# A bidirectional state-space scan rewritten: decay sums in PSUM, the output's parts accumulated in one bank by identity matmuls

## What is computed

```python
a_cs = jnp.cumsum(a, axis=2)
seg = a_cs[:, :, :, None] - a_cs[:, :, None, :]
decay = jnp.exp(jnp.where(lower, seg, -jnp.inf))
cb = jnp.einsum('bctgn,bcsgn->bctsg', cc, bc)
y_diag = jnp.einsum('bctsgh,bcsghp->bctghp', cb[..., None] * decay, xdt)
y_off = jnp.einsum('bctgn,bcghpn->bctghp', cc, h_in) * jnp.exp(a_cs)[..., None]
```

## Time and profile before

| | us |
|---|---|
| median of 3 runs | 1650.7 (1649.86 to 1651.47) |
| profiled execution | 1647.13 |
| its span, first to last instruction | 1645.4 |
| TensorE busy (matmul) | 1369.0, 83% |
| TensorE weight load busy | 1188.6, 72% |
| VectorE busy | 920.8, 56% |
| ScalarE busy | 693.6, 42% |
| GpSimd busy | 279.6, 17% |
| mean granted TensorE clock | 0.913 of 2.4 GHz |

### The profile page before, as it was taken

The page is one execution under the profiler, slowest core; times in us unless marked ns, Lnnn a source line. Parts: engine busy times, 40 slices in busy tenths (PEclk is TensorE's granted clock), DMA queues, the critical chain, the costliest instruction groups (busy, mean ns, idle before and its releaser), DMA issues. The chain is left out here.

```text
span 1645.4 us, 20520 instructions
## 1 busy us (share of the span) xinstructions
PE 1369.0 (83%) x7697; PEld 1188.6 (72%) x7697; DVE 920.8 (56%) x1201; ACT 693.6 (42%) x1186; POOL 279.6 (17%) x286
## 2 busy tenths in 40 slices
PE   3999989799998999787778734999974489999980
PEld 1799989799997889645555523998873378888860
DVE  2411532476762111288889868233346189999966
ACT  2423311244342221335557747111121177777753
POOL 0600000000000010256667741000004000000002
PEclk9999999899999999898889966999966799999995
DMA  9972211121213331511111131332435589999945
GB/s 385 406 305 77 76 53 52 59 74 57 78 52 109 118 134 72 170 52 39 39 40 40 51 140 60 115 101 92 162 153 195 201 314 408 406 412 413 413 186 204
DMA packets 55498, 267.96 MB, mean 163 GB/s; under 512 B 7467, under 2 KB 11763, under 8 KB 35062
## 3 DMA queue, kind: packets, MB, share of 16 engines
q1 hardware_dynamic: 42806, 221.21, 35.8%
q0 software_dynamic: 12608, 45.62, 7.1%
HBM read 218.54 MB, written 48.27 MB: 162 GB/s over the span
## 5 line engine op out<-in xcount | busy, mean ns | idle before, releaser
L212 PE MATMUL banks<-rounded,rounded 128*128 128x320 f32 (+1 forms) x1168 | 366.5, 314 | 20.2 <-PEq L1266 6.8
L213 PE MATMUL banks<-rounded,rounded 128*128 128x320 f32 (+1 forms) x1168 | 364.5, 312 | 0.0
L214 PE MATMUL banks<-rounded,rounded 128*128 128x320 f32 (+1 forms) x1168 | 364.4, 312 | 0.0
L191 DVE TENSOR_TENSOR rounded<-words,rounded 128x2048 fp32r<-128x2048 f32 x52 | 119.2, 2292 | 226.5 <-ACT rounded L183 224.3
L212 PEld LDWEIGHTS banks<-rounded,rounded 128*128 128x128 f32 (+1 forms) x1168 | 221.5, 190 | 21.8 <-issue 14.4
L1849 DVE TENSOR_TENSOR rounded<-words,rounded 128x2048 fp32r<-128x2048 f32 x93 | 212.9, 2290 | 34.3 <-ACT rounded L1840 33.4
L213 PEld LDWEIGHTS banks<-rounded,rounded 128*128 128x128 f32 (+1 forms) x1168 | 221.5, 190 | 0.4
L214 PEld LDWEIGHTS banks<-rounded,rounded 128*128 128x128 f32 (+1 forms) x1168 | 221.3, 189 | 0.4
L1840 ACT ACTIVATE rounded<-words 128x2048 fp32r<-128x2048 f32 x96 | 183.7, 1917 | 48.0 <-PE banks L1967 40.7
L183 ACT ACTIVATE rounded<-words 128x2048 fp32r<-128x2048 f32 x52 | 99.2, 1909 | 141.0 <-PE banks L233 62.6
L231 PE MATMUL banks<-rounded,rounded 128*128 128x512 f32 x280 | 112.1, 400 | 10.7 <-PEq L632 6.6
(11 more groups left out here) (269 smaller groups left out, 2227.7 us busy)
## 6 DMA issues: line engine op xcount, KB each, us to landing
words<-in_units SPq DMA_DIRECT2D x52, 1024.0 KB, 5.0
words<-in_wg SPq DMA_DIRECT2D x32, 1024.0 KB, 7.4
words<-in_wu SPq DMA_DIRECT2D x32, 1024.0 KB, 7.5
words<-in_wd SPq DMA_DIRECT2D x32, 1024.0 KB, 8.3
words<-in_w_mod_rest SPq DMA_DIRECT2D x32, 512.0 KB, 4.9
slot_rows<-words POOLq DMA_DIRECT2D x27, 512.0 KB, 22.9
expert_rows<-words POOLq DMA_DIRECT2D x25, 512.0 KB, 9.0
words<-in_w_mod SPq DMA_DIRECT2D x4, 2048.0 KB, 22.5
```

The source lines that it names most:

```text
L191: self.nc.vector.tensor_tensor(self.lo[:, i % 2, :], self.raw[:, i % 2, :], self.hi[:, i % 2, :].bitcast(F32), ALU.subtract).then_inc(self ...
L212: nc.tensor.matmul(out, lhs[0](k), rhs[0](k), start=(k == 0), stop=False)
L213: nc.tensor.matmul(out, lhs[0](k), rhs[1](k), start=False, stop=False)
L214: last = nc.tensor.matmul(out, lhs[1](k), rhs[0](k), start=False, stop=(k == nk - 1))
```

## The change

The scan's loop is written anew and computes the same quantities. In the diff the lines taken out of VectorE's loop, and out of ScalarE's old main loop, are left out; they stand in the listing above.

- The decays: TensorE writes into a bank for each direction first a mask of 0 and -1e30 (`shut`, through a bf16 identity), then, for each of the four heads, the running sums of `A` along the moved side: an fp32 matmul whose stationary operand is one column of `A` repeated 128 times and whose moving operand is the triangle `le` or `ge`. ScalarE takes the exponential of each head and direction, with minus the running sum (`NCS`) as its bias, into `E`. `RH`, `RL`, `AH` and the rounded triangles are gone.
- ScalarE copies the product of C and B unmasked; VectorE multiplies all eight matrices `E` of a sub-block by it in place, in one instruction. dt no longer goes into the matrix: GpSimd multiplies the rows by it, for both directions, into `XT`.
- The output of a sub-block is accumulated in one bank: the skip product through an identity matmul, eight matmuls of 64 columns (four heads, two directions), and the two scaled state terms through two identity matmuls. VectorE only scales the state terms, both in one instruction; ScalarE copies the finished bank to `X`.

```diff
-    RH, RL = kit.rnd(O_HL + 2048, 4, 512), kit.rnd(O_HL + 4096, 4, 512)
-    GX, TT = (kit.at(O_HL + 6144 + 1024 * j, 2, 512) for j in range(2))
-    M = GX
-    SO = TT
+    E = kit.at(O_HL + 2048, 6, 512)
+    XT = kit.at(O_HL + 5120, 6, 256)
+    SO = kit.at(O_HL + 6656, 2, 512)
-    gtr, ltr = kit.rnd(O_K + 1872, P), kit.rnd(O_K + 2000, P)
-    AH = kit.rnd(O_TMP + 3360, NC, 64)
+    NCS = kit.at(O_TMP + 3360, 2, NC, 32)
...
-    CB = kit.at(O_TMP + 1280, 2, 2, P)
+    CB = kit.at(O_TMP + 1280, 2, P)
+    shut = kit.at(O_TMP + 1536, P).bitcast(BF16).rearrange("p (d n) -> p d n", d=2)
+    identb = kit.at(O_TMP + 1664, P // 2).bitcast(BF16)
...
-            def decays(j):
+            def time_rows(j):
                 c, g, q = subs[j]
-                if j >= 2:
-                    pool.wait_ge(seg_done, j - 1)
-                for d, mask in ((0, le), (1, ge)):
-                    hs = heads4(g, q)
-                    av = A[:, c, 32 * d + hs.start:32 * d + hs.stop]
-                    nc.gpsimd.tensor_tensor(byhead(RL[:, 2 * d + j % 2, :], 4), av.unsqueeze(2).broadcast_to([P, 4, P]),
-                                            mask.unsqueeze(1).broadcast_to([P, 4, P]), ALU.mult).then_inc(low_decays, 1)
-            def finish_y(j):
-                c, g, q = subs[j]
-                pool.wait_ge(y_steps, ev(j + 1))
-                nc.gpsimd.tensor_tensor(X[:, c, g * GW + q * 256:g * GW + (q + 1) * 256], V1[:, j % 2, :],
-                                        OF[:, j % 2, 1, :], ALU.add).then_inc(y_whole, 1)
+                if j >= 3:
+                    pool.wait_ge(y_done, j - 2)
+                hs = heads4(g, q).start
+                rows = byhead(X[:, c, g * GW + q * 256:g * GW + (q + 1) * 256], 4)
+                dt = DT[:, c, :].rearrange("p (d h) -> p d h", d=2)[:, :, hs:hs + 4]
+                nc.gpsimd.tensor_tensor(XT[:, 2 * (j % 3):2 * (j % 3) + 2, :].rearrange("p d (h n) -> p d h n", h=4),
+                                        rows.unsqueeze(1).broadcast_to([P, 2, 4, HD]),
+                                        dt.unsqueeze(3).broadcast_to([P, 2, 4, HD]), ALU.mult).then_inc(rows_timed, 1)
 
...
             for j, (c, g, q) in enumerate(subs):
-                if j + 2 < NS:
-                    decays(j + 2)
                 if j in x_at:
                     weigh(pool, nc.gpsimd, x_at[j])
                 if j >= 2:
-                    pool.wait_ge(y_steps, ev(j - 1))
+                    pool.wait_ge(y_done, j - 1)
                 nc.gpsimd.tensor_tensor(byhead(YK[:, j % 2, :], 4), byhead(X[:, c, g * GW + q * 256:g * GW + (q + 1) * 256], 4),
                                         DSK[:, heads4(g, q)].unsqueeze(2).broadcast_to([P, 4, HD]),
                                         ALU.mult).then_inc(skip_ready, 1)
-                if 2 <= j < NL + 2:
-                    finish_y(j - 2)
+                if j + 2 < NS:
+                    time_rows(j + 2)
 
...
             def prepare(j):
                 c, g, q = subs[j]
-                pe.wait_ge(low_decays, 2 * j + 2)
-                if j >= 2:
-                    pe.wait_ge(seg_exp, j - 1)
-                pe.wait_ge(high_decays, 8 * (j + 1))
-                for n, (mask, R) in enumerate(((gtr, RH[:, j % 2, :]), (gtr, RL[:, j % 2, :]),
-                                               (ltr, RH[:, 2 + j % 2, :]), (ltr, RL[:, 2 + j % 2, :]))):
-                    last = nc.tensor.matmul(ps[:, j % 2, :], mask, R, start=(n == 0), stop=(n == 3))
-                last.then_inc(seg_done, 1)
+                for d, mask in ((0, le), (1, ge)):
+                    if j:
+                        pe.wait_ge(decays_done, 8 * j - 4 + 4 * d)
+                    nc.tensor.matmul(ps[:, d, :].rearrange("p (h n) -> p h n", h=4), identb,
+                                     shut[:, d, :].unsqueeze(1).broadcast_to([P, 4, P]), start=True, stop=False)
+                    for h in range(4):
+                        n = 32 * d + heads4(g, q).start + h
+                        last = nc.tensor.matmul(ps[:, d, h * P:(h + 1) * P], A[:, c, n:n + 1].broadcast_to([P, P]), mask,
+                                                start=False, stop=(h == 3))
+                    last.then_inc(sums_spread, 1)
...
-                    pe.wait_ge(y_steps, ev(j - 1))
+                    pe.wait_ge(off_scaled, min(j - 1, NL))
+                    pe.wait_ge(y_steps, j - 1)
...
                     nc.tensor.matmul(ps[:, 5 + j % 2, 0:256], ct, hF[:, c - 1, w4], start=True, stop=True)
-                    nc.tensor.matmul(ps[:, 5 + j % 2, 256:512], ct, hb(c)[:, w4], start=True, stop=True)
+                    nc.tensor.matmul(ps[:, 5 + j % 2, 256:512], ct, hb(c)[:, w4], start=True, stop=True).then_inc(off_done, 1)
+                o = ps[:, 2 + j % 2, 0:256]
+                pe.wait_ge(skip_ready, j + 1)
+                nc.tensor.matmul(o, ident, YK[:, j % 2, :], start=True, stop=False)
+                pe.wait_ge(rows_timed, j + 1)
                 pe.wait_ge(matrix_ready, j + 1)
                 for h in range(4):
-                    x0 = g * GW + q * 256 + (h // 2) * P
-                    last = nc.tensor.matmul(ps[:, 2 + j % 2, h * P:(h + 1) * P], M[:, j % 2, h * P:(h + 1) * P],
-                                            X[:, c, x0:x0 + P], start=True, stop=True)
+                    for d in range(2):
+                        b = 2 * (j % 3) + d
+                        last = nc.tensor.matmul(o[:, h * HD:(h + 1) * HD], E[:, b, h * P:(h + 1) * P], XT[:, b, h * HD:(h + 1) * HD],
+                                                start=False, stop=(not c and h == 3 and d == 1))
+                if c:
+                    pe.wait_ge(off_scaled, j + 1)
+                    nc.tensor.matmul(o, ident, OF[:, j % 2, 0, :], start=False, stop=False)
+                    last = nc.tensor.matmul(o, ident, OF[:, j % 2, 1, :], start=False, stop=True)
                 last.then_inc(y_done, 1)
...
-            nc.scalar.activation(AH, A, ACT.Copy).then_inc(a_split, 1)
             act.wait_ge(sums_done, 1)
+            for n in range(2):
+                nc.scalar.activation(NCS[:, n, :, :].rearrange("p c h -> p (c h)"), ps[:, n, 0:160],
+                                     ACT.Copy, scale=-1.0).then_inc(exps_done, 1)
...
+            def take_y(j):
                 c, g, q = subs[j]
+                act.wait_ge(y_done, j + 1)
+                nc.scalar.activation(X[:, c, g * GW + q * 256:g * GW + (q + 1) * 256], ps[:, 2 + j % 2, 0:256],
+                                     ACT.Copy).then_inc(y_steps, 1)
+
+            for j, (c, g, q) in enumerate(subs):
+                if j >= 3:
+                    act.wait_ge(y_done, j - 2)
+                for d in range(2):
+                    if d and q == 0:
+                        gi = j // 2
+                        act.wait_ge(cb_done, gi + 1)
+                        if gi >= 2:
+                            act.wait_ge(matrix_ready, 2 * (gi - 1))
+                        nc.scalar.activation(CB[:, gi % 2, :], ps[:, 4, (gi % 2) * P:(gi % 2 + 1) * P], ACT.Copy).then_inc(cb_taken, 1)
+                    act.wait_ge(sums_spread, 2 * j + d + 1)
+                    for h in range(4):
+                        n = heads4(g, q).start + h
+                        nc.scalar.activation(E[:, 2 * (j % 3) + d, h * P:(h + 1) * P], ps[:, d, h * P:(h + 1) * P], ACT.Exp,
+                                             bias=NCS[:, d, c, n:n + 1]).then_inc(decays_done, 1)
                 if j >= 2:
-                    act.wait_ge(seg_done, j - 1)
-                for d, mask in ((0, le), (1, ge)):
-                    for h in range(4):
-                        hs = 32 * d + heads4(g, q).start + h
-                        nc.scalar.activation(RH[:, 2 * d + j % 2, h * P:(h + 1) * P], mask, ACT.Copy,
-                                             scale=AH[:, c, hs:hs + 1].bitcast(F32)).then_inc(high_decays, 1)
-
-            act.wait_ge(a_split, 1)
-            decays(0)
-            decays(1)
+                    take_y(j - 2)
+            take_y(NS - 2)
+            take_y(NS - 1)
...
+            for d, mask in ((0, le), (1, ge)):
+                nc.vector.tensor_scalar(shut[:, d, :], mask, BIG, -BIG, ALU.mult, ALU.add).then_inc(shut_ready, 1)
+            nc.vector.tensor_copy(identb, kit.const("ident")).then_inc(shut_ready, 1)
+            dve.wait_ge(exps_done, 4)
...
+            def scale_off(j):
                 c, g, q = subs[j]
                 if j >= 2:
                     dve.wait_ge(y_done, j - 1)
+                dve.wait_ge(off_done, j + 1)
+                scale = EX.rearrange("p (d a) c h -> p d a c h", d=2)[:, :, 0, c, heads4(g, q)]
+                nc.vector.tensor_tensor(OF[:, j % 2, :, :].rearrange("p d (h n) -> p d h n", h=4),
+                                        ps[:, 5 + j % 2, :].rearrange("p (d h n) -> p d h n", d=2, h=4),
```

(48 more changed lines are left out.)

55 lines of the change are left out of this document (6 added, 49 removed).

## The result

| | us |
|---|---|
| before, median of 4 runs | 1650.9 (1649.9 to 1651.5) |
| changed kernel, median of 4 runs | 1703.9 (1701.2 to 1705.5) |
| ratio | 1.0320, 95% interval 1.0302 to 1.0338 |
| profiled execution of the changed kernel, and its span | 1701.18, 1699.4 |

A forecast was written before the change was run, and what follows sets the result against it. TensorE was to replace VectorE's chain as the loop's bound: 292.6 us of work plus 2 of waiting against 244.6, +50.0, and front +1.9, sum +51.9, giving 1702 us; own case 1688 to 1716, 8-in-10 range 1665 to 1728.

The forecast's parts named there:

- TensorE becomes the bound: In the scan's loop, TensorE's work of 292.6 us exceeds the present loop of 244.6 us, where VectorE led.
- A record costs 0.11 however few columns it moves: In TensorE's fp32 matmuls, loading 128 stationary columns sets 0.11 us per record; 64 moved columns do not halve it.
- The rest of the sum: TensorE's loop work beyond the record price: all terms sum to 292.6 us, 294.6 with 2 us of waiting.
- It does not wait for off_scaled: Before the state terms' identity matmuls, VectorE's scaling arrives in time, with about 1 us to spare.
- the new-wait rival: In the loop, identity matmuls wait 0.6 us each for VectorE's late scaling: +20, 1722 us; chance 0.08.
- The clock at 1.00: TensorE's mean granted clock in the loop is 1.00, as the waits that accompany 0.87 go.
- the rival at 0.87: TensorE's clock in the loop stays at 0.87, 292.6 us become 336: +44, 1746 us; chance 0.06.
- sixes among nines: The prediction's reading of TensorE's clock row in the old profile, for stage_ssd, slices 16 to 23.
- Front +1.9, end 0: Before the loop, two copies precede the exponential's table load, +1.9 us; at the end, a ScalarE copy replaces two adds, 0.
- Short records are short: In the diagonal, a 64-column record costs half, 0.055 us: 36 us less, 1666 us; chance 0.10.
- both kinds cost half: Records with a repeated-column stationary and those with 64 moved columns cost 0.055 us: 1631 us; chance 0.04.
- No difference: In the loop, the added matmuls disappear in TensorE's idle time; chance 0.02.

The follow-up runs named there:

- half_moved: In the changed kernel, the eight diagonal matmuls of a sub-block move 32 columns instead of 64; 1702.3 us.
- half_stationary: In the changed kernel, seven of the eight diagonal matmuls of a sub-block load 64 stationary columns instead of 128, still moving 64; 1684.9 us.
- log_dt: In the changed kernel, dt's logarithm goes into the exponential's bias, VectorE adds both directions' matrices, and four diagonal matmuls replace eight; 1667.2 us.
- both: In the changed kernel, dt's logarithm in the bias with four diagonal matmuls, and the identity matmuls' sums given back to VectorE and GpSimd; 1621.2 us.

## Why the prediction was right, point by point

- *TensorE becomes the bound*: right. 54.00 of 54 us busy, and taking work from it gave back its price in the loop one for one (45.7 for 45, 34.7 for 34.6).
- *A record costs 0.11 however few columns it moves*: right for the size (0.108 and 0.111), and half_moved shows it apart from everything else. The reason given, the load of the stationary, is borne out by half_stationary, but not that the price is in proportion to the loaded columns: 64 take 0.072, not 0.054. The forecast needed only 128, so the sum did not suffer. It is also not the only price: the group L1059 of the earlier trace rows, 2 columns loaded and 128 moved, takes 1.84 / 16 = 0.115 a record (880.76 to 882.60 in its timeline), so for the decay sums, which load 128 and move 128, the trace can't say which side sets the 0.111. The rule of the Trainium skill ("TensorE: Matmul & The Clock Gate", "LDWEIGHTS (loading the stationary operand)"), a time by columns, holds here at 128 and would give 53 ns for 64, where the 14 short records show 72 each. The table in its section "Back-to-back issue gap" gives about 60 cycles for 1 to 64 columns as the gap of matmuls without loads between them; with a load for every record it doesn't apply, as the prediction said: 0.106 with 32 columns.
- *The rest of the sum*: 292.6 was forecast for TensorE's work. With the measured parts it is 32 x 6.16 + 8 x (2.21 + 0.43 + 1.73) + 4.4 + 19 x 2.14 + 12 x 0.95 = 288.5. The loop is 297.5, not 294.6; the missing waits are 9 us, not 2. Nine gaps ahead of the modulation group L1048, behind ScalarE's copy L1131 of the CB product, make 5.7 of them. The prediction costed no such wait, though the earlier trace rows shows the same place waiting in the kernel before (2.21 us for L1198). In the 16 sub-blocks with a state part that have a modulation group, the first state term behind the group takes 0.53 instead of 0.43, 1.6 us. The rest is the start and the end of the loop.
- *It does not wait for off_scaled*: right. No such wait of TensorE stands among the waits; the new-wait rival is out.
- *The clock at 1.00*: right in every window of the loop; the rival at 0.87 is out. The prediction's "sixes among nines" in the old clock row is misread: it has eights in slices 18 to 20 and a single six, in slice 23.
- *Front +1.9, end 0*: the table measured +1.8, and 0.8 came on top by the clock; behind the loop 1.7 us came back that the prediction did not have.
- *The number*: nearer than its terms. The errors are -4.1 in TensorE's work, +7 in its waits, +0.8 at the front and -1.7 behind the loop; they add up to +2.0 on a forecast of +51.9, where the span grew by 54.0. The mechanism carries the forecast; that it is only 2 us off is partly luck.
- *Short records are short; both kinds cost half*: out by the records' spacing. *No difference*: out by the measured time.

## What to carry to other kernels

Before sums are moved onto TensorE through identity matmuls, ask which engine ends last once the rest of the rewrite is done: fp32 through the identity cost 0.43 us for 256 columns here, and VectorE, with its time more than halved, could have done the same adds unseen. Splitting a product into more and narrower fp32 matmuls isn't free although the moved columns stay the same: count stationary loads of 128 columns, two for each fp32 matmul, at 0.11 each. And a factor per row of an exponential's matrix, here dt, can go into the bias as a logarithm, which for one more addition on VectorE made one matmul of two.

## What was not expected

- A record with half a stationary costs two thirds of one with a whole: 0.072 for 64 columns against 0.108 for 128, and with 32 moved columns in place of 64 the group of 16 records still takes 1.17 us against 1.23.
- The gains of two edits on the bound engine added within 1 us in the loop (218.0 for 217.1), although VectorE's busy time in the window 725 to 800 rose from 29.87 of 75 us in log_dt to 49.84 in both. That the medians agree within half a microsecond (1621.2 and 1620.8) is luck; the runs of both alone lie 3.5 us apart.
- A stationary that is one column repeated 128 times costs no more than others: 0.111 per record with 128 moved columns, where L1095 before had 0.10 to 0.115.
- Ahead of the loop the same 32 records of the context states (L1013 in the changed kernel) took 5.4, 5.9 or 6.7 us in different kernels, with TensorE's clock rising sooner or later.
